# Square sums of the query heads on GpSimd instead of TensorE, in a two-layer decoder trunk on one Trainium2 core

## The chip, the core and the metric

The kernel runs on one core of a Trainium2 chip. A core has five engines that run side by side and meet only at semaphores: TensorE (PE; matrix products into PSUM banks; its weight loads are listed as PEld), VectorE (DVE), ScalarE (ACT), GpSimd (POOL) and SyncE (SP, which here only issues transfers). The metric is the device time of one launch in microseconds (us); lower is better.

## The reference, cut to what matters

Two layers work on x of 256 tokens by 2048 channels. Layer 0 holds a pooling mixer and block attention (MoBA) side by side, layer 1 holds sparse attention with an indexer (DSA) and a convolution module. Each layer projects a normalised, modulated x by a wide weight matrix. The change touches one thing in it, the root mean square norm of each query head over its 128 channels:

```
def _rms(x, g):
    x32 = x.astype(jnp.float32)
    y = x32 * lax.rsqrt(jnp.mean(x32 * x32, axis=-1, keepdims=True) + EPS)
    return (y * g.astype(jnp.float32)).astype(x.dtype)

    q = _rms(q.reshape(B_, S, N_HEADS, HEAD_DIM), moba_qn[e])   # layer 0; 8 heads of 128
    q = _rms(q.reshape(B_, S, N_HEADS, HEAD_DIM), dsa_qn[o])    # layer 1; 8 heads of 128
```

So for each of 2 x 8 heads and each of 256 tokens the sum of 128 squares is needed. It scales a row of the attention scores, so it is not needed before the first scores.

## The kernel before, in words

**Slabs.** All projections are cut into 141 slabs of 128 output channels. SP loads a slab as two halves of 512 KB (`load_slab`, L297 and L301). ACT rounds each half to the upper part `whi` (`hi`, L496), DVE subtracts to get the lower part `wlo` (`lo`, L1204), and TensorE forms a slab from 16 x 3 = 48 products of 256 columns (`slab`, L835 to L837; `slab_v`, L980 to L983, for keys and values) into one of two PSUM banks `Z[0]`, `Z[1]`, in turn. ACT and DVE work `AHEAD` = 2 slabs in front of TensorE. Between its slab work DVE also adds the modulation units `acc` (L1214, L1231), which SP streams from HBM.

**Order.** Each engine has its own list, written out by hand, which it goes through strictly in order; a wait holds back everything behind it on that engine. The first 12 slabs of layer 0 are worked together into six banks (`unsplit_chunk`); four of them are query heads 0 to 3. Slabs 12 to 15 are query heads 4 to 7 of layer 0, slabs 16 to 23 its keys, 24 to 31 its values. In layer 1 slabs 85 to 92 are the query heads, 93 to 100 the keys, from 101 on the values.

**Query heads.** ACT copies a query head with its channels on the partitions (tokens in the free dimension) from PSUM to `X` (L534, L658), squares it into a tile of 128 x 256 (L536, L659), and so frees the bank (`z_free`, for heads 0 to 3 `q_read`). For slabs 12 to 15 and 85 to 92 the square goes to `T[w % 2]`; heads 0 to 3 of layer 0 take `T[0]`, `T[1]`, `SG[0]`, `SG[1]`. TensorE then sums over the 128 partitions: a product for each half of the tokens, with the squares as weights and a column of ones (`qk_stats`, L943, called behind the next slab; L1093 for heads 0 to 3, in front of slab 13). The result is a column of bank `M` with the tokens on the partitions, and `qk_stat` is raised.

**Who reads the sums.** At the first value slab (24, 101) DVE waits for all 8 heads and computes the reciprocal roots of queries and keys (`rsqrt`, L1261 to L1273). Attention follows.

**GpSimd** has little to do: it clears the accumulators (`clear`, L391), issues some transfers (L413, L425, L432, L460), scales the position bias (`slopes`, L399), and adds squares of the new x at the end of layer 0 (L420). Its helper `own` issues an instruction and then waits for its completion.

**The small records.** One fp32 product shows as two records in the trace, so a head's two sums show as four (x4). Slabs' products show as one record each.

Of the kernel before, what the change touches and what calls it, by code (L numbers as in the profile page):

```python
# [11 lines left out]
P = 128  # L12
# [3 lines left out]
KC = D_MODEL // P  # L16
HC = HALF // P
QT = SEQ // P
# [81 lines left out]
def build(nc, xT, params, pool_w, w_slabs, ada_units, x1_dram, outT):  # L100
    ctx = ExitStack()
    with ctx:
# [49 lines left out]
        rc = sb("rc", [P, 16])  # L152
        psum = [ctx.enter_context(nc.psum_tensor(f"bank{i}", [P, 512], F32)) for i in range(8)]
# [41 lines left out]
        qk_stat = sem("qk_stat")  # L195
# [169 lines left out]
        def _(pool):  # L365
# [26 lines left out]

            def slopes(layer, heads=range(HC)):
# [38 lines left out]
            pool.dma_start(PW, pool_w).then_inc(pw_in, 16)  # L432
            clear(6)
# [26 lines left out]
            pool.dma_start(KI[IDX_DIM:2 * IDX_DIM, :], KW[0:IDX_DIM, :]).then_inc(ki_in, 16)  # L460
            pool.wait_ge(mask_ready, 1)
# [14 lines left out]
        def _(act):  # L476
# [54 lines left out]
            def evict_qk(w, t, q0, kind, layer):  # L531
# [3 lines left out]
                               Z[w % 2][:, 0:SEQ], ACT.Copy, scale=gain)  # L535
                act.activation(T[:, w % 2, :], Z[w % 2][:, 0:SEQ], ACT.Square).then_inc(z_free[w % 2], 1)  # L536

            def evict_k(w, k0):
                pair = (w - k0) // 2
                if (w - k0) % 2:  # L540
# [3 lines left out]
                                   bank[:].rearrange("p (a b) -> p a b", a=QT), ACT.Copy)  # L544
                    if pair:
                        b = (k0 + pair - 1) % 2
                        act.wait_ge(z_free[b], (k0 + 1 - b) // 2 + 1 + 2 * ((pair - 1) // 2 + 1))
# [113 lines left out]
            act.wait_ge(qk_stat, 4)  # L661
# [152 lines left out]
        def _(pe):  # L814
# [124 lines left out]
            def qk_stats(w, t, q0):  # L939

                pe.wait_ge(z_free[w % 2], bank_uses(w, t) + 2)
                for q in range(QT):
                    ins = mm(M[:, bass.ds(q * KC + now(w, t) - q0, 1)], T[:, w % 2, q * P:(q + 1) * P],  # L943
                             ones[:, 0:1], start=True, stop=True)
                ins.then_inc(qk_stat, 1)

# [136 lines left out]
            def slab_stat(q0):  # L1083
                def step(w, t):
                    slab_h(w, t)
                    qk_stats(w - 1, t, q0)
                return step

            slab_h(12, None)
            for i in range(4):  # L1090
                pe.wait_ge(q_read, i + 1)
                for q in range(QT):
                    ins = mm(M[:, q * KC + i:q * KC + i + 1], (T, SG)[i // 2][:, i % 2, q * P:(q + 1) * P],  # L1093
                             ones[:, 0:1], start=True, stop=True)
                ins.then_inc(qk_stat, 1)
# [708 lines left out]
```

## Time and profile before

| | |
|---|---|
| median of 3 runs | 983.06 us (979.67 to 984.81) |
| span of the profiled execution (first to last instruction) | 977.3 us |
| TensorE busy | 942.7 us (96%) |
| VectorE busy | 822.4 us (84%) |
| ScalarE busy | 422.5 us (43%) |
| GpSimd busy | 63.5 us (6%), 76 instructions |
| mean granted TensorE clock | 0.991 of full speed |
| DMA | 261.26 MB, mean 267 GB/s |

The span runs from the first to the last instruction of one execution; that execution's own launch time is not given apart from it, and the three timed runs lie 2.4 to 7.5 us above the span. Products of TensorE overlap in the records: a slab product has a record of 0.28 us but a new one starts every 0.12 us. For TensorE the start times are therefore read, not the durations. The granted clock is 1.00 at 2.4 GHz and 0.50 at 1.2 GHz.

### The profile page before, as it was taken

What the parts mean: (1) busy time and instruction counts of PE and PEld (TensorE: products, weight loads), DVE (VectorE), ACT (ScalarE), POOL (GpSimd) and SP (SyncE); (2) the same over time, 40 slices, a digit from 0 to 9 for tenths busy, and PEclk for the clock granted to TensorE, in tenths of its full rate; (3) what the DMA queues carried; (4) which work ended last, traced back from release to release, by engine and by line L of the source; (5) the groups of instructions that cost most, each with busy time, mean ns of one, the idle gap of its engine ahead of it and who ended that gap; (6) DMA issues with size and microseconds to landing.
All of it is one profiled execution on the core that took longest, in us unless ns stands there. A gap on an engine that the chain in (4) does not pass through costs nothing.

```text
span 977.3 us, 18750 instructions
## 1 busy us (share of the span) xinstructions
PE 942.7 (96%) x7042; PEld 908.3 (93%) x7042; DVE 822.4 (84%) x1256; ACT 422.5 (43%) x726; POOL 63.5 (6%) x76
## 2 busy tenths in 40 slices
PE   2999999999999999999999999999999999999998
PEld 2887889999998999999999999999999989998887
DVE  5887968887999778999887999888999986879964
ACT  2220125444655444444444444444556655743331
POOL 1000000010110000132100000000011100000000
PEclk9999998999999999999999999999999999999999
DMA  9999988888876878899959555544455445587962
GB/s 366 409 399 399 379 298 319 293 329 330 325 286 233 294 260 312 322 370 377 339 176 321 193 176 189 175 151 140 164 175 193 172 163 203 199 315 288 360 227 75
DMA packets 77666, 261.26 MB, mean 267 GB/s; under 512 B 7952, under 2 KB 8592, under 8 KB 77344
## 3 DMA queue, kind: packets, MB, share of 16 engines
q1 hardware_dynamic: 72384, 240.90, 67.5%
q10 hardware_dynamic: 2880, 10.49, 2.7%
q0 software_dynamic: 2336, 8.98, 2.6%
q8 instruction: 43, 0.70, 0.3%
q14 instruction: 23, 0.19, 0.1%
HBM read 256.07 MB, written 4.19 MB: 266 GB/s over the span
## 4 chain that ended last, share of the span: by engine, by line
PE 72%; DVE 19%; DMA 4%; issue 2%; ACT 2%; SPq 1%; DVEq 0%; ACTq 0%
PE bank L835 13%; PE bank L836 13%; PE bank L837 13%; PE bank L856 6%; DVE wlo L1204 5%; PE bank L893 4%; PE bank L980 4%; DVE acc L1214 4%; PE bank L983 4%; PE bank L982 4%; PE bank L854 3%; DMA Y<-ada_units 3%; DVE Y L1431 2%; PE bank L927 2%; DVE acc L1234 1%
## 5 line engine op out<-in xcount | busy, mean ns | idle before, releaser
L496 ACT ACTIVATE whi<-raw 128x1024 fp32r<-128x1024 f32 x256 | 270.1, 1060 | 382.3 <-PE bank L837 217.0
L1204 DVE TENSOR_TENSOR wlo<-raw,whi 128x1024 fp32r<-128x1024 f32 x256 | 312.0, 1234 | 74.9 <-ACT whi L496 73.6
L835 PE MATMUL bank<-hhi,whi 128*128 128x256 f32 x912 | 263.8, 289 | 2.5 <-ACT T L741 0.9
L836 PE MATMUL bank<-hlo,whi 128*128 128x256 f32 x912 | 259.3, 284 | 0.0
L837 PE MATMUL bank<-hhi,wlo 128*128 128x256 f32 x912 | 259.1, 284 | 0.0
L1214 DVE SCALAR_TENSOR_TENSOR acc<-ada,cact,acc 128x1024 f32<-128x1024 f32 x144 | 187.4, 1302 | 23.9 <-DMA ada<-ada_units 12.6
L835 PEld LDWEIGHTS bank<-hhi,whi 128*128 128x128 f32 x912 | 176.2, 193 | 5.3 <-issue 3.1
L836 PEld LDWEIGHTS bank<-hlo,whi 128*128 128x128 f32 x912 | 176.2, 193 | 0.1
L837 PEld LDWEIGHTS bank<-hhi,wlo 128*128 128x128 f32 x912 | 176.1, 193 | 0.0
L980 PE MATMUL bank<-whi,hhi 128*128 128x256 f32 x512 | 146.7, 287 | 0.0
L982 PE MATMUL bank<-whi,hlo 128*128 128x256 f32 x512 | 144.9, 283 | 0.0
L983 PE MATMUL bank<-wlo,hhi 128*128 128x256 f32 x512 | 144.9, 283 | 0.0
L980 PEld LDWEIGHTS bank<-whi,hhi 128*128 128x128 f32 x512 | 98.2, 192 | 0.8 <-issue 0.7
L1431 DVE SCALAR_TENSOR_TENSOR Y<-U,par,Y 128x256 f32<-128x256 f32 x240 | 98.6, 481 | 0.0
L982 PEld LDWEIGHTS bank<-whi,hlo 128*128 128x128 f32 x512 | 98.3, 192 | 0.1
L983 PEld LDWEIGHTS bank<-wlo,hhi 128*128 128x128 f32 x512 | 98.2, 192 | 0.0
L856 PE MATMUL bank<-both_g,whi 128*128 128x512 f32 x256 | 89.9, 399 | 0.0
L893 PE MATMUL bank<-X,raw 128*128 128x256 f32 x384 | 86.5, 387 | 1.6 <-DMA raw<-w_slabs 1.5
L893 PEld LDWEIGHTS bank<-X,raw 128*128 128x128 f32 x384 | 74.2, 195 | 12.2 <-issue 1.8
L835 PE MATMUL bank<-both_g,whi 128*128 128x256 f32 x256 | 73.1, 286 | 0.0
L836 PE MATMUL bank<-both_g,whi 128*128 128x256 f32 x256 | 72.5, 283 | 0.0
L837 PE MATMUL bank<-both_g,wlo 128*128 128x256 f32 x256 | 72.4, 283 | 0.0
(195 smaller groups left out, 1220.2 us busy)
## 6 DMA issues: line engine op xcount, KB each, us to landing
raw<-w_slabs SPq DMA_DIRECT2D x260, 512.0 KB, 4.5
ada<-ada_units SPq DMA_DIRECT2D x160, 512.0 KB, 6.6
raw<-w_slabs ACTq DMA_DIRECT2D x20, 512.0 KB, 7.0
V<-ada_units SPq DMA_DIRECT2D x16, 512.0 KB, 9.7
Y<-ada_units SPq DMA_DIRECT2D x16, 512.0 KB, 11.3
X<-xT SPq DMA_DIRECT2D x1, 2048.0 KB, 12.6
x_dram<-X POOLq DMA_DIRECT2D x4, 512.0 KB, 8.5
outT<-X POOLq DMA_DIRECT2D x3, 512.0 KB, 4.9
```

What stands on the lines that cost most here:

```text
L496: act.activation(whi[:, slot], raw[:, slot], ACT.Copy).then_inc(hi_done, 1)
L835: mm(out, whi[:, s, k, :], ahi[:, c, :], start=(c == 0), stop=False)
L836: mm(out, whi[:, s, k, :], alo[:, c, :], start=False, stop=False)
L837: last = mm(out, wlo[:, s, k, :], ahi[:, c, :], start=False, stop=(c == KC - 1))
L856: last = mm(out[:], whi[:, s, k, :], flat(both_g[:, c]), start=(c == 0), stop=(c == KC - 1), skip_group_check=True)
L893: last = mm(wide(s), raw[:, slot, k, :], X[:, c, :], start=(c == 0 and s % 2 == 0), stop=(c == KC - 1), skip_group_check=True)
L980: mm(out, hhi[:, c, tokens], upper, start=(c == 0 and q == 0), stop=False, skip_group_check=True)
L982: mm(out, hlo[:, c, tokens], upper, start=False, stop=False, skip_group_check=True)
L983: last = mm(out, hhi[:, c, tokens], lower, start=False, stop=(c == KC - 1), skip_group_check=True)
L1204: dve.tensor_tensor(wlo[:, s], source, whi[:, s].bitcast(F32), ALU.subtract)\
L1214: dve.scalar_tensor_tensor(acc[:, p % 2, :], unit_at(first + u), cact[:, bass.ds(k, 1)], acc[:, p % 2, :], ALU.mult, ALU.add).then_inc(ada ...
L1431: ins = dve.scalar_tensor_tensor(Y[:, j, :], U[:, j, k:k + SEQ], par[:, wcol:wcol + 1], Y[:, j, :], ALU.mult, ALU.add)
```

## The change

The sums over the partitions leave TensorE. For each query head GpSimd runs one `partition_all_reduce` (add) in place on the 128 x 256 tile of squares, waits for it, and issues two transfers, one for each half of the tokens, that move 128 numbers of partition 0 (512 bytes) into one column of a new SBUF tile `qsum`, 4 bytes into each of 128 partitions. Their landing raises one of four semaphores `q_sum`, one for each tile of squares (`T[0]`, `T[1]`, `SG[0]`, `SG[1]`). ACT waits for that semaphore before it overwrites a tile of squares, where it waited before only for the bank or (once, L661) for `qk_stat`. DVE waits for all `q_sum` at slabs 24 and 101 and reads `qsum` where it read bank `M`. In GpSimd's list the eight heads of layer 0 stand between the load of `PW` and `clear(6)`, those of layer 1 between the transfer to `KI` and `slopes(1)`.

```diff
+        qsum = sb("qsum", [P, 2, QT, HC])
...
-        qk_stat = sem("qk_stat")
+        q_sum = [sem(f"q_sum{i}") for i in range(4)]
...
+            def q_stats(layer, h, squared, home):
+                own(pool.partition_all_reduce(squared, squared, P, bass.bass_isa.ReduceOp.add))
+                for q in range(QT):
+                    pool.dma_start(qsum[:, layer, q, h:h + 1], squared[0:1, q * P:(q + 1) * P]).then_inc(q_sum[home], 16)
...
             pool.dma_start(PW, pool_w).then_inc(pw_in, 16)
+            for h in range(4):
+                pool.wait_ge(q_read, h + 1)
+                q_stats(0, h, (T, SG)[h // 2][:, h % 2, :], h)
+            for w in range(WIDE[0], K0):
+                pool.wait_ge(z_free[w % 2], w // 2 + 2)
+                q_stats(0, w - Q0, T[:, w % 2, :], w % 2)
             clear(6)
...
+            for w in range(Q1, K1):
+                pool.wait_ge(z_free[w % 2], w // 2 + 2)
+                q_stats(1, w - Q1, T[:, w % 2, :], w % 2)
             pool.wait_ge(mask_ready, 1)
             slopes(1)
...
@@ evict_qk (ACT)
+                h = w - q0
+                if layer == 0 or h >= 2:
+                    uses = (h - 2) // 2 if layer == 0 else 3 + h // 2
+                    act.wait_ge(q_sum[w % 2], 16 * QT * uses)
                 act.activation(T[:, w % 2, :], Z[w % 2][:, 0:SEQ], ACT.Square).then_inc(z_free[w % 2], 1)
@@ evict_k (ACT)
+                    if k0 == K0 and not pair:
+                        act.wait_ge(q_sum[2], 16 * QT)
+                        act.wait_ge(q_sum[3], 16 * QT)
@@ heads 0 to 3 (ACT)
-            act.wait_ge(qk_stat, 4)
             evict_qk(12, None, Q0, "q", 0)
@@ TensorE
-            def qk_stats(w, t, q0):
-                pe.wait_ge(z_free[w % 2], bank_uses(w, t) + 2)
-                for q in range(QT):
-                    ins = mm(M[:, bass.ds(q * KC + now(w, t) - q0, 1)], T[:, w % 2, q * P:(q + 1) * P],
-                             ones[:, 0:1], start=True, stop=True)
-                ins.then_inc(qk_stat, 1)
...
             slab_h(12, None)
-            for i in range(4):
-                pe.wait_ge(q_read, i + 1)
-                for q in range(QT):
-                    ins = mm(M[:, q * KC + i:q * KC + i + 1], (T, SG)[i // 2][:, i % 2, q * P:(q + 1) * P],
-                             ones[:, 0:1], start=True, stop=True)
-                ins.then_inc(qk_stat, 1)
             slab_h(13, None)
-            qk_stats(12, None, Q0)
-            slab_stat(Q0)(14, None)
+            slab_h(14, None)
             pool_product(0)
-            slab_stat(Q0)(15, None)
+            slab_h(15, None)
...
             for w in range(86, K1):
-                slab_stat(Q1)(w, None)
+                slab_h(w, None)
                 logits(w - 86)
@@ attention_step (DVE)
-                    dve.wait_ge(qk_stat, HC * (layer + 1))
+                    for home, uses in enumerate((3 + 4 * layer, 3 + 4 * layer, 1, 1)):
+                        dve.wait_ge(q_sum[home], 16 * QT * uses)
-                    rsqrt(2 * layer + 1, 2 * KC, M[:, 0:2 * KC], P, ksum[:])
+                    rsqrt(2 * layer + 1, 2 * KC, qsum[:, layer, :, :], P, ksum[:])
```

## Rows read from the trace of the kernel before

**Rows 1.** Page, part 4: the chain that ended last, share by engine

```profile
PE 72%; DVE 19%; DMA 4%; issue 2%; ACT 2%; SPq 1%; DVEq 0%; ACTq 0%
```

**Rows 2.** Waits of PE, 140 to 240 us: who for whom, us, times, longest

```profile
PE bank L1093 <- ACT T L659: 1.0, 1, 1.0
```

**Rows 3.** Windows: stretch, length, busy us of PE, PEld, DVE, ACT, POOL, clock, DMA share

```profile
146.90:150.90 4.00, 2.98 (x20) 2.53 (x18) 2.79 (x3) 4.00 (x12) 0.00 (x0) 0.86 0.86 342
150.90:156.70 5.80, 5.80 (x28) 5.80 (x29) 5.63 (x6) 1.84 (x5) 0.00 (x0) 0.51 0.94 335
...
206.70:208.30 1.60, 1.60 (x16) 1.60 (x16) 1.50 (x2) 1.06 (x1) 0.00 (x0) 1.00 0.97 366
...
480.00:485.00 5.00, 4.78 (x41) 4.59 (x40) 2.19 (x10) 1.92 (x5) 1.43 (x2) 0.93 1.02 413
...
618.00:681.00 63.00, 63.00 (x501) 60.23 (x500) 54.99 (x108) 27.32 (x42) 0.00 (x0) 1.00 0.44 153
```

**Rows 4.** Timeline of PE: start us, us, instruction, [idle before <-releaser]

```profile
146.74 0.28 PE L836 MATMUL bank<-hlo,whi 128*128 128x256 f32 x1
146.86 0.28 PE L837 MATMUL bank<-hhi,wlo 128*128 128x256 f32 x1
...
150.88 0.56 PE L835 MATMUL bank<-hhi,whi 128*128 128x256 f32 x1
...
156.58 0.31 PE L837 MATMUL bank<-hhi,wlo 128*128 128x256 f32 x1
...
165.45 0.50 PE L943 MATMUL bank<-ones,T 128*128 128x1 f32 x4
165.81 1.97 PE L955 MATMUL bank<-Y,V 128*128 128x256 f32 x8
167.43 0.47 PE L835 MATMUL bank<-hhi,whi 128*128 128x256 f32 x1
...
206.50 1.84 PE L927 MATMUL bank<-ones,acc 128*128 128x1 f32 x16
...
624.57 0.50 PE L943 MATMUL bank<-ones,T 128*128 128x1 f32 x4
624.99 0.49 PE L1041 MATMUL bank<-KW,QI 64*128 64x128 f32 x2
```

**Rows 5.** Timeline of ACT: the square of head 0

```profile
147.61 0.44 ACT L659 ACTIVATE T<-bank 128x256 f32<-128x256 f32 x1
```

**Rows 6.** Timeline of DVE, 145 to 202 us

```profile
145.99 2.67 DVE L1214 SCALAR_TENSOR_TENSOR acc<-ada,cact,acc 128x1024 f32<-128x1024 f32 x2 [2.04 <-DMA ada<-ada_units]
...
154.66 1.22 DVE L1204 TENSOR_TENSOR wlo<-raw,whi 128x1024 fp32r<-128x1024 f32 x1
...
171.84 1.23 DVE L1204 TENSOR_TENSOR wlo<-raw,whi 128x1024 fp32r<-128x1024 f32 x1 [1.70 <-ACT whi L496]
...
178.04 1.23 DVE L1204 TENSOR_TENSOR wlo<-raw,whi 128x1024 fp32r<-128x1024 f32 x1 [1.25 <-ACT whi L496]
...
199.08 2.35 DVE L1204 TENSOR_TENSOR wlo<-raw,whi 128x1024 fp32r<-128x1024 f32 x2
```

**Rows 7.** POOL: two groups by line (busy us, mean ns), one line's durations (ns min/median/max)

```profile
L420 POOL TENSOR_TENSOR SP<-SP,T 128x256 f32<-128x256 f32 x13 | 17.8, 1369 | 56.5 <-ACT T L691 56.5
L413 POOL DMA_DIRECT2D V<-xT x2 | 1.1, 575 | 29.3 <-PE bank L1028 29.3
L399 POOL TENSOR_SCALAR DS<-MK x8: 1169/1172/2082, 713.6 to 779.3; 128x384 f32<-128x384 f32 x8
```

**Rows 8.** Timeline of DVE at two instructions that run beside one of POOL

```profile
404.56 3.15 DVE L1214 SCALAR_TENSOR_TENSOR acc<-ada,cact,acc 128x1024 f32<-128x1024 f32 x2
...
713.44 2.66 DVE L1204 TENSOR_TENSOR wlo<-raw,whi 128x1024 fp32r<-128x1024 f32 x2
```

**Rows 9.** DMA issues of POOL: count, KB each, median us from issue to landing

```profile
U<-xT POOLq DMA_DIRECT2D x2, 512.0 KB, 8.8
...
KI<-KW POOLq DMA_DIRECT2D x1, 64.0 KB, 2.6
```

More of the change, by code:

```diff
@@ L1081, in _ @@
             unsplit_chunk(15)
[L1083 to L1087, printed above, removed]
-            slab_h(12, None)
-            for i in range(4):
-                pe.wait_ge(q_read, i + 1)
-                for q in range(QT):
-                    ins = mm(M[:, q * KC + i:q * KC + i + 1], (T, SG)[i // 2][:, i % 2, q * P:(q + 1) * P],
-                             ones[:, 0:1], start=True, stop=True)
-                ins.then_inc(qk_stat, 1)
+            slab_h(12, None)
             slab_h(13, None)
-            qk_stats(12, None, Q0)
-            slab_stat(Q0)(14, None)
+            slab_h(14, None)
             pool_product(0)
-            slab_stat(Q0)(15, None)
+            slab_h(15, None)
             for w in range(K0, V0):
                 slab_v(w, K0, keys=True)
-                if w == K0:
-                    qk_stats(w - 1, None, Q0)
                 if w < K0 + 2:
@@ L1158, in _ @@
                 if w == K1:
-                    qk_stats(w - 1, None, Q1)
                     logits(w - 86)
@@ L1261, in rsqrt @@
                     seq(dve.tensor_scalar(parts[:, :, HC:KC], keys, 1.0 / count, EPS, ALU.mult, ALU.add))
-                    a, src = parts[:, :, 0:HC], src.rearrange("p (q n) -> p q n", q=QT)[:, :, 0:HC]
+                    a = parts[:, :, 0:HC]
                     settle()
```

## The prediction

> **What bounds the kernel now.** I read the chain of waits first: TensorE holds 72% of it, DVE 19% [rows 1]. Then TensorE's waits in the stretch where the change begins: one only, 1.0 us, on ACT's squares of head 0 [rows 2]. So from 140 to 240 us TensorE is the bound, with a product started every 0.12 us (146.74 to 146.86) [rows 4]; a slab of 48 takes 5.8 us. The windows then show what the eye misses in the busy shares: while the sums of heads 0 to 3 run, the granted clock is 0.86, and in the 5.8 us behind them 0.51, which is the 1.2 GHz level [rows 3]. In layer 1 (618 to 681 us) TensorE is busy all the time and DVE for 54.99 of 63.00 us [rows 3]. What TensorE no longer issues is thus saved as long as DVE and the new waits keep up; those two are the question.
>
> **What goes, layer 0.** The last product of slab 12 starts at 146.86, so slab 13 could start at 146.98; it starts at 150.88 [rows 4]. That is 3.9 us, one wait and 16 one-column products with their doubled records. Then come 26 steps of slab 13 up to 156.58, 5.70 us where 26 x 0.12 = 3.1 would do: 2.6 us for the low clock. Four more heads are summed behind slabs 13 to 16, each from 165.45 to 165.81 or alike, 0.36 us: 1.4 us. Together 7.9 us.
>
> **What goes, layer 1.** Eight times from 624.57 to 624.99, 0.42 us [rows 4]: 3.4 us.
>
> **What comes: the custom instruction.** No row shows a reduction over partitions. From below it cannot beat a pass over 256 numbers per partition; the nearest row is GpSimd's own addition of two 128x256 tiles, 1.37 us [rows 7], and I take 1.4 us. From above: if the sum passes through the engine like eight such additions in a row, 8 x 1.37 = 11 us. For each transfer GpSimd's issue costs 0.58 us [rows 7], and I add 0.1 us for the completion wait: 1.4 + 0.1 + 1.15 = 2.65 us a head. A landing takes 2.6 us for 64 KB in a calm stretch (DMA share 0.44), 8.8 us for 512 KB in a full one [rows 3, 9]; here the share is 0.85 to 0.94 and the piece tiny, but 128 pieces of 4 bytes. I take 3.5 us, with 2.6 and 8.8 as ends.
>
> **The new wait that counts.** Head 0's squares are ready at 147.61 + 0.44 = 148.05 [rows 5]. Reduced 149.5, second transfer issued at 150.2, landed 153.7; with the ACT square of slab 12 (0.4) and two hand-overs bank Z[0] is free at about 154.6. Without the sums TensorE has finished slab 13 at 146.98 + 5.8 = 152.8, so it waits 1.9 us for slab 14. Behind ACT's waiting square stand its copies of slab 15's weights, which DVE does not reach before the pooling work behind 154.66 [rows 6]: no cost. The clock: 1.6 us of 16 one-column products at 206.7 left it at 1.00, the 4 us from 146.9 brought it down, the 5 us from 480 to 0.93 already inside [rows 3]. A gap of 1.9 us is like the first, so I charge nothing; if it falls all the same, 2.6 us. The later ones: head h of layer 0 is issued by 148.1 + 2.65 (h + 1), head 4 lands at about 164.3 and head 5 at 167. Their tiles are wanted by slab 14's and 15's squares, whose banks TensorE needs back only at slabs 16 (about 167.9) and 18. No wait. Slab 14 then ends at 154.6 + 5.8 = 160.4, not 165.45. With the other three sums that makes 7.9 - 1.9 = 6.0 us by slab 17.
>
> **What DVE lets through.** Slab 20's second half starts at 206.50 - 24 x 0.12 = 203.6 on TensorE; its lower part is written at 199.08 + 1.2 = 200.3 [rows 4, 6]: 3.3 us in hand. From 151 us to there DVE has only 1.70 + 1.25 us idle, both waiting for ACT [rows 6], which TensorE's earlier pace moves up. So TensorE can gain at most 3.3 + 2.95 = 6.3 us here, less what GpSimd takes from DVE. That price stands in two rows: beside the longest `slopes` (2.08 us, median 1.17; 384 numbers read) DVE's pair of subtractions took 2.66 us and not 2.35, 0.31 us [rows 6 to 8]; beside a two-input addition (512 read) a pair of units took 3.15 and not 2.67, 0.48 us. By numbers read, 256 cost about 0.2 us; eight heads 1.6 us (3.8 at 0.48). Layer 0 keeps 6.3 - 1.6 = 4.7 us. In layer 1 DVE's 8.0 us idle covers 3.4 + 1.6 us, ACT's wait for the tile of two heads ago has 7 us for each slab against 2.65, and DVE's wait at slab 101 comes long after. GpSimd's own list suffers nothing: it is idle in both places, and what stands behind is `clear(6)` and the bias, not due until about 208 us and 713 us.
>
> **Two rules of the Trainium skill that speak against the change.** The trace has GpSimd and DVE losing parts of a microsecond beside each other, 0.31 and 0.48 us [rows 8]. The skill's page SBUF — State Buffer, section "Who interferes with whom", says more: the pair of ports they share is an exclusive lock, held for the whole instruction; the other engine stands still. The trace does not agree: an addition of 1.37 us cost DVE 0.48. It is rival three.
> No row here prices a sum over partitions. The GPSIMD Engine Reference, section "Cross-partition — where GPSIMD wins", gives 247,699 ns for a partition-axis reduction of [128, 2048]; an estimate by it for 256 columns is 31 us a head, and by it the sum would be rival four's, about 1320 us. The same page, section "Instruction dispatch", has a first call of loaded code pay about 6 us; the sum stays the same if that falls into GpSimd's idle time before the first head.
>
> **Sum.** 4.7 + 3.4 = 8.1 us less. Both reckonings are differences inside the profiled execution (span 977.3 us); put on the median of 983.06, which is 5.8 us above that span, they give 975.0 us. The forecast's own range is 968 to 980.
>
> **Rivals.**
> 1. *The landing eats layer 0's gain.* With 8.8 us from issue to landing Z[0] is free at 159.5, about the 159.6 of before; TensorE has stood 6.7 us, the clock falls and 2.6 us are lost again; 1.4 us of sums remain, so layer 0 loses about 1 us, layer 1 gains 3.4: 980.6 us. For it: the full DMA engines, 4-byte pieces. Against: 2.6 us at KI. A reduction of 3 us does nearly the same.
> 2. *The custom instruction is slow (slower than before).* Place: squares of slab 14, which wait for head 4, fifth in GpSimd's line; TensorE needs that bank at 173.7 as of before. It decides from 148.1 + 5 (t + 1.25) - 0.6 + 3.5 + 0.4 = 173.7, t = 3.2 us, on. At t = 11: head 4 lands at 212.3, slab 16 is 39 us late. In layer 1 the first square is ready at about 626.5 (624.6 and 2 us for ACT) and one more follows every 7.1 us, the eighth at 676; at 12.25 us a head it has to wait for head 5, 626.5 + 6 x 12.25 + 2.9 = 703: 26 us. 983 + 65 = 1048 us. For it: nothing bounds it in the trace. Against: nothing in one pass over 256 columns resembles eight.
> 3. *DVE stands still for the whole reduction.* Eight times 1.4 = 11.2 us against 6.3 in hand makes layer 0 4.9 us longer; in layer 1 11.2 against 8.0 idle is 3.2 more: 991 us.
> 4. *A reduction that goes through the numbers one by one, 31 us a head* (the page's rule above). Eight heads with their issues take 261 us. DVE's wait at the first value slab comes some 80 us behind head 0 in layer 0 (12 slabs of 5.8 us and the small products between them) and some 100 us in layer 1 (16 slabs): 180 + 160 us longer, about 1320 us. For it: only that the sum over partitions has no row. Against: each of GpSimd's rows of this size is under 2.1 us [rows 7].
>
> **How the numbers follow.** Forecast 55%, rival one 25%, two 10%, three 8%, four 2%. A measurement of this kernel tells 0.5%, 4.9 us, from no change. Of the forecast's case a tenth (its upper end, 978 to 980) falls within that; faster 0.50, within 0.30, slower 0.20. The range for 8 in 10 takes the forecast's and rival one's: 968 to 988.
>
> **What would show it.** No L943 or L1093; slab 13 starts at 147.0 and the clock stays at 1.00 up to 160; TensorE's longest new wait is 1 to 3 us before slab 14, on ACT's square, and that on a transfer. GpSimd shows 16 custom instructions whose spacing to the first transfer is 1.4 us; DVE's L1204 mean stays below 1.27 us. If slab 16 starts later than 173.7, rival two or one holds; if L1204 stretches by more than 1 us beside GpSimd, rival three. An unchanged start of slab 16 and a gain in layer 1 alone would make the forecast wrong by its larger term.

## The result, and the profile after

| | before | after |
|---|---|---|
| median of 20 runs | 981.02 us (976.79 to 984.81) | 984.30 us (981.22 to 991.29) |
| ratio, 95% interval | | 1.0036 [1.0021, 1.0052] |
| span of the profiled execution | 977.3 us | 982.7 us |
| mean granted TensorE clock | 0.991 | 0.991 |

The kernel became 3.5 us slower, where 8 us less were forecast. The predicted range held the time; the sign was wrong. TensorE issues less, and the kernel is no faster for it.

The page of the kernel after: part 1, engine busy, and part 4, the chain that ended last.

```profile
span 982.7 us, 18682 instructions
PE 937.6 (95%) x6978; PEld 901.3 (92%) x6978; DVE 835.7 (85%) x1256; ACT 422.5 (43%) x726; POOL 118.2 (12%) x124
...
PE 56%; DVE 30%; DMA 7%; issue 4%; ACT 2%; SPq 1%; DVEq 0%; ACTq 0%
```

DVE is busy 835.7 us where it was 822.4, though the change gives it no work; its share of the chain rises from 19% to 30% [rows 1]. The waits of TensorE from 140 to 240 us (who for whom: us, times, longest) say the same. [rows 2] shows one before, 1.0 us, on ACT; a second, 0.8 us for ACT's `U` at 140 us, is in both kernels:

```profile
PE bank L968 <- DVE Y L1362: 3.1, 2, 2.5
PE bank L993 <- DVE wlo L1201: 2.9, 2, 1.5
PE bank L856 <- DVE wlo L1201: 2.6, 2, 2.0
PE bank L856 <- ACT U L672: 1.0, 2, 0.8
```

The first three, 8.6 us, are for DVE: for the pooled operand `Y` and for lower parts of weights. The windows of the kernel after, with the columns of [rows 3]:

```profile
146.90:150.90 4.00, 2.85 (x24) 2.64 (x23) 3.25 (x3) 4.00 (x12) 2.16 (x2) 1.00 0.68 274
150.90:156.70 5.80, 4.91 (x28) 4.91 (x29) 5.70 (x4) 3.07 (x6) 5.43 (x6) 0.71 0.63 200
156.70:178.00 21.30, 17.25 (x132) 16.29 (x130) 20.85 (x24) 8.66 (x14) 16.54 (x18) 1.00 0.71 243
178.00:212.00 34.00, 31.46 (x251) 30.84 (x250) 32.89 (x40) 14.42 (x32) 0.78 (x2) 1.00 0.86 310
618.00:681.00 63.00, 63.00 (x491) 59.28 (x490) 61.65 (x109) 29.01 (x44) 30.17 (x25) 1.00 0.50 164
```

TensorE's first new wait is not the one forecast, before slab 14 on ACT's square. It stands in the middle of slab 13, for DVE's lower part of the second half, and the clock is 0.71 right behind it (150.90 to 156.70), where 1.00 was forecast:

```profile
151.79 0.52 PE L856 MATMUL bank<-hhi,whi 128*128 128x256 f32 x1 [2.05 <-DVE wlo L1201]
```

From 156.70 to 178.00 DVE is busy 20.85 of 21.30 us with 24 instructions; before, 17.86 us for the same number:

```profile
156.70:178.00 21.30, 21.30 (x174) 21.09 (x173) 17.86 (x24) 9.89 (x15) 0.00 (x0) 1.00 0.85 303
```

So the instructions of DVE grew longer. Which ones, the timelines show. GpSimd first, after:

```profile
148.43 1.81 POOL L395 PARTITION_ALL_REDUCE T<-T  x1 [19.32 <-ACT T L681]
...
151.87 1.74 POOL L395 PARTITION_ALL_REDUCE T<-T  x1
...
155.03 1.82 POOL L395 PARTITION_ALL_REDUCE SG<-SG  x1
...
158.26 1.76 POOL L395 PARTITION_ALL_REDUCE SG<-SG  x1
...
161.43 1.74 POOL L395 PARTITION_ALL_REDUCE T<-T  x1
...
164.59 1.96 POOL L395 PARTITION_ALL_REDUCE T<-T  x1
...
168.84 2.27 POOL L395 PARTITION_ALL_REDUCE T<-T  x1 [0.91 <-ACT T L555]
...
174.47 2.39 POOL L395 PARTITION_ALL_REDUCE T<-T  x1 [1.99 <-ACT T L555]
```

And DVE, after, in the same stretch:

```profile
146.35 1.28 DVE L1211 SCALAR_TENSOR_TENSOR acc<-ada,cact,acc 128x1024 f32<-128x1024 f32 x1 [3.06 <-DMA ada<-ada_units]
148.38 2.22 DVE L1211 SCALAR_TENSOR_TENSOR acc<-ada,cact,acc 128x1024 f32<-128x1024 f32 x1 [0.74 <-DMA ada<-ada_units]
150.53 3.47 DVE L1201 TENSOR_TENSOR wlo<-raw,whi 128x1024 fp32r<-128x1024 f32 x2
153.92 3.31 DVE L1211 SCALAR_TENSOR_TENSOR acc<-ada,cact,acc 128x1024 f32<-128x1024 f32 x2
...
158.29 1.61 DVE L1349 TENSOR_TENSOR SP<-U 128x542 f32<-128x542 f32 x1
159.94 0.69 DVE L1356 SCALAR_TENSOR_TENSOR Y<-SP,U 128x512 f32<-128x512 f32 x1
...
160.93 1.63 DVE L1362 TENSOR_TENSOR Y<-SP,U 128x2 f32<-128x2 f32 x2
...
163.62 3.31 DVE L1211 SCALAR_TENSOR_TENSOR acc<-ada,cact,acc 128x1024 f32<-128x1024 f32 x2
...
167.99 0.71 DVE L1349 TENSOR_TENSOR SP<-U 128x542 f32<-128x542 f32 x1
...
169.49 1.47 DVE L1356 SCALAR_TENSOR_TENSOR Y<-PTs,U 128x512 f32<-128x512 f32 x1
...
171.25 0.24 DVE L1362 TENSOR_TENSOR Y<-PTs,U 128x4 f32<-128x4 f32 x2
...
175.13 3.25 DVE L1201 TENSOR_TENSOR wlo<-raw,whi 128x1024 fp32r<-128x1024 f32 x2
```

Eight reductions, and eight rows of DVE that are too long, each where a reduction runs. Against the same forms undisturbed (1.28, 0.71, 0.69 and 0.24 above; 2.35 and 2.67 in [rows 6]) the excess is 0.94, 1.12, 0.64, 0.90, 1.39, 0.64, 0.78 and 0.90 us: 7.3 us, 0.91 for each reduction. The reductions grow as well: the first six take 1.74 to 1.96 us, the last two 2.27 and 2.39.

In layer 1 the same is seen in one group, the taps of the convolution, after. Columns: busy us, mean ns, idle before.

```profile
L1428 DVE SCALAR_TENSOR_TENSOR Y<-U,par,Y 128x256 f32<-128x256 f32 x240 | 105.3, 506 | 0.0
```

The same group before:

```profile
L1431 DVE SCALAR_TENSOR_TENSOR Y<-U,par,Y 128x256 f32<-128x256 f32 x240 | 98.6, 481 | 0.0
```

105.3 less 98.6 is 6.7 us for eight reductions, 0.84 each. It lies in DVE's idle time: 61.65 of 63.00 us are busy there, 54.99 before [rows 3].

**Where the time went.** A shift table says at which slab the kernel after falls behind. I read it from the start of DVE's subtraction for the first half of each slab: start in the kernel, less its start at slab 12, less the same difference in the kernel before. It rests on one profile of each kernel. Negative is earlier.

| kernel | slab 16 | 20 | 28 | 52 | 84 | 124 | ratio of the timed runs |
|---|---|---|---|---|---|---|---|
| after | +6.95 | +4.73 | +3.80 | +3.79 | +8.56 | +6.22 | 1.0036 [1.0021, 1.0052] |
| e1_no_sums | -0.07 | -2.27 | -0.54 | -0.54 | -0.94 | -3.60 | 0.9973 [0.9956, 0.9990] |
| e3_no_reduce | +0.06 | -3.09 | -4.01 | -4.03 | -3.55 | -6.23 | 0.9969 [0.9953, 0.9986] |
| e4_write_only | -0.13 | -2.72 | -3.16 | -3.16 | -1.52 | -4.17 | 0.9951 [0.9935, 0.9966] |
| e12_read_copy | +3.29 | +1.41 | +2.15 | +2.15 | +3.02 | +0.35 | 0.9994 [0.9972, 1.0017] |
| e2_own_tiles | +7.59 | +5.36 | +6.09 | +6.09 | +6.26 | +4.14 | 1.0067 [1.0042, 1.0092] |
| e5_twice | +8.18 | +9.80 | +11.18 | +11.18 | +12.63 | +17.94 | 1.0189 [1.0166, 1.0213] |
| e6_layer0 | +5.51 | +3.36 | +2.42 | +2.42 | +2.86 | +3.18 | 1.0055 [1.0033, 1.0077] |
| e7_layer1 | +0.64 | -0.80 | -0.80 | -0.80 | +1.51 | -0.69 | 0.9989 [0.9974, 1.0004] |
| e8_late_sums | -0.08 | -3.17 | -4.11 | -4.12 | -3.24 | -3.25 | 0.9988 [0.9972, 1.0003] |
| e11_both | -0.03 | -3.02 | -3.95 | -3.96 | -3.25 | -5.44 | 0.9959 [0.9941, 0.9977] |
| e13_side_eight | +5.04 | +2.80 | +3.47 | +3.47 | +4.10 | +4.12 | 1.0045 [1.0019, 1.0072] |
| e14_side_four | +2.59 | -0.55 | -0.93 | -0.93 | +0.60 | +0.61 | 1.0000 [0.9978, 1.0021] |
| e15_late_side | +5.15 | +2.91 | +1.98 | +1.98 | +4.72 | +4.74 | 1.0025 [1.0000, 1.0050] |

In the kernel after 3.80 us are lost by slab 28 (layer 0) and 2.3 won in layer 1 (slab 84 to 124). Some 4.8 more are lost between slabs 52 and 84, where nothing of the change runs; `e6_layer0` loses 0.4 there. The trace shows on what: the clock of 460 to 480, 480 to 500 and 500 to 530 us is 0.91, 0.91 and 0.94 in the kernel after, 1.00, 0.91 and 1.00 before. By length times what is missing that is 3.6 us more lost, and TensorE has a new wait of 2.0 us for DVE's `X` there. Why the clock fell twice more is not shown; `e4`, with 0.91 and 0.94 in the last two of these stretches, has one such fall more than before and runs well below it.

The table is coarse to a microsecond or two in another way: it rests on one execution each, and for `e3`, `e6`, `e8` and `e11` that was the fastest one timed. The ratios decide.

A second table shows DVE alone, from the start of its first subtraction for slab 12 to the end of the third pooled operand (before: the rows at 186.16). How much later that operand and TensorE's product on it come than before is again counted from slab 12.

| kernel | GpSimd in it | DVE busy | DVE idle | operand | product |
|---|---|---|---|---|---|
| before | nothing | 41.35 | 12.28 | 0 | 0 |
| e3_no_reduce | transfers only | 41.24 | 9.31 | -3.07 | -4.11 |
| e4_write_only | 8 `memset` | 41.24 | 9.68 | -2.71 | -3.16 |
| e8_late_sums | nothing | 41.20 | 9.26 | -3.17 | -4.21 |
| e12_read_copy | 8 pairs of copies | 45.25 | 9.80 | +1.42 | +0.38 |
| e14_side_four | 4 reductions | 44.20 | 8.89 | -0.54 | -0.93 |
| e13_side_eight | 8 reductions | 47.79 | 8.65 | +2.81 | +1.77 |
| e15_late_side | 8 reductions | 47.84 | 8.71 | +2.91 | +1.87 |
| e6_layer0 | 8 reductions | 48.59 | 8.41 | +3.37 | +2.33 |
| after | 8 reductions | 48.43 | 9.94 | +4.73 | +3.69 |
| e2_own_tiles | 8 reductions | 48.96 | 10.03 | +5.36 | +4.32 |
| e5_twice | 16 reductions | 54.94 | 8.49 | +9.80 | +8.76 |

DVE does the same work in all of them. Without an instruction of GpSimd that reads SBUF it takes 41.2 to 41.4 us, with four reductions 2.9 us more, with eight 6.4 to 7.6 more, with sixteen 13.6 more: 0.7 to 0.95 us each. In the kernel after 1.8 us of the lateness are DVE's longer waits for modulation units before 148.4 us (3.06 + 0.74, before 2.04); `e6` does not have them, so they are not laid to the change.

### The profile page after: what moved, and what is told of

Same layout as the page of the kernel before. It is cut to its first block, busy times and chain, and to the rows that moved or that the text cites. A ratio compares the mean times of both kernels' runs of the same rounds, so it can differ in the third digit from the quotient of the medians.

```text
span 982.7 us, 18682 instructions
## 1 busy us (share of the span) xinstructions
PE 937.6 (95%) x6978; PEld 901.3 (92%) x6978; DVE 835.7 (85%) x1256; ACT 422.5 (43%) x726; POOL 118.2 (12%) x124
## 4 chain that ended last, share of the span: by engine, by line
PE 56%; DVE 30%; DMA 7%; issue 4%; ACT 2%; SPq 1%; DVEq 0%; ACTq 0%
PE bank L856 9%; PE bank L857 9%; PE bank L858 9%; DVE wlo L1201 9%; DVE acc L1211 7%; PE bank L877 6%; DVE Y L1428 6%; DMA ada<-ada_units 6%; PE bank L914 4%; PE bank L993 3%; PE bank L995 3%; PE bank L996 3%; PE bank L875 3%; PE bank L948 2%; DMA Y<-ada_units 1%
## 5 line engine op out<-in xcount | busy, mean ns | idle before, releaser
L1211 DVE SCALAR_TENSOR_TENSOR acc<-ada,cact,acc 128x1024 f32<-128x1024 f32 x144 | 189.8, 1318 | 30.4 <-DMA ada<-ada_units 19.4
L1428 DVE SCALAR_TENSOR_TENSOR Y<-U,par,Y 128x256 f32<-128x256 f32 x240 | 105.3, 506 | 0.0
```

What stands on the lines that cost most here:

```text
L1211: dve.scalar_tensor_tensor(acc[:, p % 2, :], unit_at(first + u), cact[:, bass.ds(k, 1)], acc[:, p % 2, :], ALU.mult, ALU.add).then_inc(ada ...
L1428: ins = dve.scalar_tensor_tensor(Y[:, j, :], U[:, j, k:k + SEQ], par[:, wcol:wcol + 1], Y[:, j, :], ALU.mult, ALU.add)
```

## The experiments

Each was timed in 5 rounds beside the kernel before. `e1`, `e3`, `e4` and `e12` leave the sum over the partitions out and `e5` makes it 128 times too large, so their query norms are not the reference's. Differences in microseconds are taken from the ratios, since the kernel before ran beside each group anew. The diffs are cut to their core.

**Is it the reduction, the transfers, or the saving itself?** `e1_no_sums` has neither reductions nor transfers; `e3_no_reduce` keeps the transfers and the waits for them.

```diff
 # e3_no_reduce (e1_no_sums also replaces the two transfers by a semaphore increment)
-                own(pool.partition_all_reduce(squared, squared, P, bass.bass_isa.ReduceOp.add))
```

> The changed kernel without any sums: no reduction, no transfer, no products of TensorE; qsum holds a constant (the norms of the query heads are left out). It prices what TensorE stood to gain. Theory P (GpSimd's reductions take the port from DVE and make DVE late) and theory W (ACT waits for the transfers to land) both expect 7 to 11 us below the kernel before, a ratio of 0.989 to 0.993, slab 13 starting right behind slab 12 and no drop of the clock. Rival H (the time of the one-column products was hidden anyway, DVE or the loads being the next bound): under 3 us below.

> The changed kernel without the 16 reductions, with its 32 transfers and all waits (the sums are left out; partition 0's squares are moved). Theory P: DVE's two-input instructions keep their 1.21 and 1.28 us and nearly all of e1's gain comes, 6 to 10 us below before. Theory W: the reductions were 1.8 of 4 to 6 us from square to landing, so most of the wait stays, 0 to 3 us below before.

Measured: 979.38 and 977.10 us against 980.84. With no sums at all the kernel is only 2.6 us faster, so 8 us were not there to be won: both theories had expected 7 to 11, and rival H holds. And without the reductions alone the loss becomes a gain: 0.9969 against 1.0036, 6.6 us. `e3` itself is 3.0 us below the kernel before, less than theory P expected and at the edge of theory W's range; so its time alone does not tell the two apart. DVE's busy time does (41.24 us, as without sums), and `e2` below. The transfers and their waits are not what costs. How the gain is capped shows at the third pooling product. Before, its operand from DVE, and the product:

```profile
186.16 0.24 DVE L1365 TENSOR_TENSOR Y<-SP,U 128x8 f32<-128x8 f32 x2
```

```profile
187.50 1.89 PE L955 MATMUL bank<-Y,V 128*128 128x256 f32 x8
```

DVE has it ready at 186.40, TensorE comes at 187.50: 1.1 us in hand, and 2.95 us of DVE's idle time before it [rows 6]. More than 1.1 + 2.95 = 4.05 us can't be won there. `e3`, DVE and then TensorE:

```profile
182.60 0.24 DVE L1361 TENSOR_TENSOR Y<-SP,U 128x8 f32<-128x8 f32 x2
```

```profile
182.90 1.99 PE L967 MATMUL bank<-Y,V 128*128 128x256 f32 x8 [2.52 <-DVE Y L1361]
```

TensorE waits 2.52 us for DVE there, and at slab 28 the kernel is 4.01 us ahead. The same row after, where TensorE's list is the same and DVE is late:

```profile
190.45 1.99 PE L968 MATMUL bank<-Y,V 128*128 128x256 f32 x8 [2.54 <-DVE Y L1362]
```

In `e1` the wait was longer, and the clock of 178 to 212 us fell to 0.90 (it is 1.00 in the kernel before); of 2.27 us won by slab 20, 0.54 are left at slab 28:

```profile
187.75 3.78 PE L967 MATMUL bank<-Y,V 128*128 128x256 f32 x8 [3.47 <-DVE Y L1361]
```

```profile
178.00:212.00 34.00, 30.53 (x225) 29.56 (x224) 30.78 (x38) 14.15 (x31) 0.58 (x1) 0.90 0.85 308
```

**Is it that GpSimd is busy, or that it reads?** `e4_write_only` puts a `memset` of 1920 columns, about as long as a reduction, in its place; `e12_read_copy` two copies of 384 columns from `D`.

```diff
 # e4_write_only
-                own(pool.partition_all_reduce(squared, squared, P, bass.bass_isa.ReduceOp.add))
+                own(pool.memset(both_g[:].rearrange("p a b t -> p (a b t)").bitcast(F32)[:, 0:1920], 1.0))
 # e12_read_copy: in its place, twice
+                own(pool.tensor_copy(scr[:], D[:]))
```

> As the changed kernel, but each reduction is replaced by a memset of 1920 columns of an idle tile, which keeps GpSimd busy for about as long (951 ns for 1024 columns, so 1.8 us) and reads nothing; transfers and waits stay (the sums are left out). Theory P in its form 'the reduction's reads collide with DVE's second SBUF input': DVE keeps its durations, and the time is e3's within 2 us (head 0 lands 1.8 us later). If the mere time from square to landing, or GpSimd's work of any kind, were the cost: the changed kernel's time within 1.5 us.

> The changed kernel with each reduction replaced by two copies of the 384 columns of D into a scratch tile, which keep GpSimd busy for about as long as a reduction (0.5 us for 256 columns, so 0.75 each) and read SBUF, unlike e4's memset (the sums are left out). Theory P (any GpSimd instruction that reads SBUF takes time from DVE's two-input instructions): 2 to 6 us above e4 and its DVE durations stretched. If only the custom instruction does it: e4's time within 1.5 us, DVE's durations as in before.

Measured: `e4` 976.48 us, 4.8 below the kernel before; `e12` 980.45 us, 4.2 above `e4`. The taps in `e4`, then the copies and the taps in `e12` (busy us, mean ns):

```profile
L1428 DVE SCALAR_TENSOR_TENSOR Y<-U,par,Y 128x256 f32<-128x256 f32 x240 | 98.6, 479 | 0.0
```

```profile
L396 POOL COPY scr<-D 128x384 f32<-128x384 f32 x16 | 16.6, 1036 | 52.6 <-ACT T L557 34.2 <-ACT T L683 18.2
```

```profile
L1430 DVE SCALAR_TENSOR_TENSOR Y<-U,par,Y 128x256 f32<-128x256 f32 x240 | 102.5, 495 | 0.0
```

In `e4` GpSimd is busy for as long as in the kernel after (1.72 us each), and DVE keeps pace with `e3` (slab 20 -2.72 and -3.09); its taps take what they took before; in `e12` they are longer again, 495 ns, and DVE is busy 3.9 us more up to the third pooled operand. So of the kinds tried the two that read SBUF (reduction and copy) slow DVE, and the one that only writes does not. `e12` also has a longer wait: TensorE stood 4.2 us once for a square of ACT whose transfer was late, so the 4.2 us between the two times are not DVE's alone. In `e4` such a wait was 3.1 us, and the kernel is still 4.8 us faster than before. On the reading side the Trainium skill, page SBUF — State Buffer, section "Who interferes with whom", agrees: a DVE instruction with two SBUF inputs contends with a GpSimd instruction that reads SBUF, not with one that only writes it.

**How much for each reduction?** `e2_own_tiles` gives the squares of layer 0 tiles of their own, so that ACT waits for no landing; `e5_twice` is `e2` with each reduction issued twice.

```diff
 # e2_own_tiles: q_stats and ACT's squares, layer 0
-                q_stats(0, h, (T, SG)[h // 2][:, h % 2, :], h)
+                q_stats(0, h, QI[:, h, :], 2)
-                q_stats(0, w - Q0, T[:, w % 2, :], w % 2)
+                q_stats(0, w - Q0, (T[:, 0, :], T[:, 1, :], KW[:], KI[:])[w - 12], 2)
 # e5_twice: as e2, and
                 own(pool.partition_all_reduce(squared, squared, P, bass.bass_isa.ReduceOp.add))
+                own(pool.partition_all_reduce(squared, squared, P, bass.bass_isa.ReduceOp.add))
```

> The changed kernel with a tile of its own for each of layer 0's eight squares (QI, T, KW, KI, all idle there), so that ACT waits for no landing in layer 0; reductions and transfers as they are. Theory W: the 6.3 us that ACT waited go and TensorE's waits in slabs 14 to 18 with them, 4 to 6 us below the changed kernel (ratio to before 0.994 to 0.998). Theory P: DVE loses about 0.9 us a reduction as before and the pooling work is as late; within 1.5 us of the changed kernel (ratio to before 1.002 to 1.005).

> The kernel with own tiles (e2) in which every reduction is issued twice in a row on its tile (the sums come out 128 times too large). It doubles the suspected cost alone, since ACT waits for no landing in layer 0. Theory P (each reduction takes about 0.5 to 0.9 us from DVE where DVE has none to give): 6 to 14 us above e2. Theory L (a fixed cost of the new path, such as loading the instruction's code or the transfers): under 2 us above e2.

Measured: `e2` 987.10 us (+6.6), `e5` 998.91 us. The landing wait, rival one, is refuted as the cause: without it nothing is won. That `e2` is worse than after is not shown; their intervals overlap from 1.0042 to 1.0052. Sixteen more reductions cost 12 us by the ratios (8.6 to 15.3 by their intervals), 0.75 each. DVE is busy 850.0 us in `e5` and 836.7 in `e2`: 13.3 us, 0.83 each.

**Which layer?** `e6_layer0` has the change in layer 0 only, `e7_layer1` in layer 1 only; the other layer keeps `qk_stats` on TensorE.

```diff
 # e7_layer1, from the kernel before; e6_layer0 is its mirror
             pool.dma_start(KI[IDX_DIM:2 * IDX_DIM, :], KW[0:IDX_DIM, :]).then_inc(ki_in, 16)
+            for w in range(Q1, K1):
+                pool.wait_ge(z_free[w % 2], w // 2 + 2)
+                q_stats(1, w - Q1, T[:, w % 2, :], w % 2)
...
-                slab_stat(Q1)(w, None)
+                slab_h(w, None)
```

> The change in layer 0 alone, layer 1 summed by TensorE as before. After e1 (all sums away: 2.7 us less) and e3/e4 against the changed kernel (reductions: 7 to 8 us more) theory P expects layer 0 to carry the larger part of the loss, since there DVE is the last to be ready for the pooling products: 2 to 5 us above before. If layer 1 carried it: within 1 us of before.

> The change in layer 1 alone. TensorE gives up 8 x 0.42 us; DVE has 8.0 us idle there of which eight reductions take about 6.7 (a run of 7 or 8 convolution taps grew by 0.8 us beside each). Theory P: the gain is just eaten or nearly, from 2 us below to 1 us above before. If the loss sat here: 3 us or more above before.

Measured: `e6` 986.02 us (+0.55%, interval 0.33 to 0.77), `e7` 979.33 us (-0.11%, -0.26 to +0.04). The loss sits in layer 0. It is larger in the timed runs of `e6`, 5.4 us, than in its profile, 2.4 at slab 28 and 3.2 at slab 124; the profiled execution was the fastest of them. Layer 1 gives about 1 us, which its interval can't tell from none; between slabs 84 and 124 its profile wins 2.2 us. The two add up to +0.44%, near the whole change's 0.36%.

**Is TensorE's saving in layer 0 worth anything while DVE is late?** `e13_side_eight` is the kernel before, with its sums left on TensorE, and eight reductions on the side in layer 0 whose result nobody reads or waits for; `e14_side_four` has the first four of them.

```diff
 # e13_side_eight, from the kernel before (the run calls own(...) through a helper, side_reduce)
             pool.dma_start(PW, pool_w).then_inc(pw_in, 16)
+            for h in range(4):
+                pool.wait_ge(q_read, h + 1)
+                own(pool.partition_all_reduce(QI[:, 0, :], D[:, 0:SEQ], P, bass.bass_isa.ReduceOp.add))
+            for w in range(WIDE[0], K0):          # not in e14_side_four
+                pool.wait_ge(z_free[w % 2], w // 2 + 2)
+                own(pool.partition_all_reduce(QI[:, 0, :], D[:, 0:SEQ], P, bass.bass_isa.ReduceOp.add))
```

> The kernel before, all its sums by TensorE, plus eight reductions by GpSimd in layer 0 at the places of the change, which read D and write the idle tile QI; no transfer, nobody waits for them. Theory Max (at the third pooling product TensorE waits for DVE; DVE has 1.1 us in hand there and 2.95 us idle before, 4.05 in all, and eight reductions take 7.8 us from it): TensorE is 3.8 us late from slab 28 on, as in the changed kernel, 3 to 5 us above before, though TensorE saved nothing. Theory Add (losses and savings simply add up): the changed kernel's loss plus the 4 us that it saved in layer 0, 7 to 9 us above before.

> As e13 with the first four reductions only (heads 0 to 3). Theory Max: 3.9 us taken from DVE's 4.05, so within 1 us of before. Theory Add: half of e13's loss, 3.5 to 4.5 us above before.

Measured: 985.34 us (1.0045) and 981.64 us (1.0000), against 982.31. Eight reductions beside a TensorE that keeps its sums cost 4.4 us by the ratios; the change in layer 0 (`e6`) costs 5.4, the whole change 3.5. If DVE's loss came on top of TensorE's time, `e13` would be 7 to 8 us late. It isn't: DVE is busy 6.4 us longer up to the third pooled operand but idle 3.6 us less, so the operand comes 2.8 us late; 1.1 us were in hand, and the product comes 1.8 us late. The 3.47 us at slab 28 have another 1.6 us in them, since the clock was low during that product:

```profile
190.34 3.59 PE L963 MATMUL bank<-Y,V 128*128 128x256 f32 x8 [2.74 <-DVE Y L1373]
```

The same product took 3.47 us in `e2` and 3.50 in `e12`, so their slab 28 has it too; in `e3` and after, behind waits of 2.52 and 2.54 us, it ran at full clock. TensorE's longest wait in `e13`, 140 to 240 us, is for the third pooled operand; the next, for head 0's square, is the one that was there before, now 1.8 us:

```profile
PE bank L963 <- DVE Y L1373: 2.7, 1, 2.7
PE bank L1101 <- ACT T L667: 1.8, 1, 1.8
```

`e14` closes it from the other side: its four reductions take 2.9 us of DVE, less than the slack, and nothing is lost.

**Can the saving be had without GpSimd?** `e8_late_sums` is the kernel before with heads 0 to 3 squared into `QI`, a tile that is free there, and their 16 products put in front of the third pooling product, where TensorE has DVE's slack to wait for anyway. `e15_late_side` adds the eight side reductions to it.

```diff
 # e8_late_sums, from the kernel before: the loop over i in range(4) moves from behind slab_h(12) to here
+                if w == K0 + 1:
+                    for i in range(4):
+                        pe.wait_ge(q_read, i + 1)
+                        for q in range(QT):
+                            ins = mm(M[:, q * KC + i:q * KC + i + 1], QI[:, i, q * P:(q + 1) * P],
+                                     ones[:, 0:1], start=True, stop=True)
+                        ins.then_inc(qk_stat, 1)
                 if w < K0 + 2:
                     pool_product(w - K0 + 1)
 # ACT: heads 0 to 3
-                act.activation((T, SG)[i // 2][:, i % 2, :], wide(8 + i), ACT.Square).then_inc(q_read, 1)
+                act.activation(QI[:, i, :], wide(8 + i), ACT.Square).then_inc(q_read, 1)
-            act.wait_ge(qk_stat, 4)
```

> The kernel before with one change of its own: heads 0 to 3 of layer 0 are squared into the idle tile QI and TensorE sums them not ahead of slab 13 but ahead of the third pooling product, where it would otherwise wait for DVE; GpSimd does nothing new. If the gain of e1 in layer 0 is the gap and the low clock at slab 13: 1 to 4 us below before, as far as DVE's pooling work lets it. If DVE holds TensorE back there whatever TensorE does: within 1 us of before.

> e8 (TensorE sums heads 0 to 3 late, 4.1 us ahead of before at slab 28 in its profile) plus the eight side reductions of e13. Theory Max: DVE sets the time, so the same as e13, 3 to 5 us above before, TensorE's saving being worth nothing. Theory Add: e13 less e8's gain, 3 to 4 us below e13.

(`e15` writes its reductions to `KI`, since `QI` is taken.) Measured: `e8` 979.21 us (0.9988), `e15` 983.99 us (1.0025). In the profile `e8` does what it should: the wait and the low clock at slab 13 are gone (clock 1.00 in both first windows), the 16 products take 1.84 us and TensorE then waits 0.15 us; 4.11 us are won by slab 28, the whole cap.

```profile
181.62 1.84 PE L1102 MATMUL bank<-ones,QI 128*128 128x1 f32 x16
183.62 1.99 PE L954 MATMUL bank<-Y,V 128*128 128x256 f32 x8 [0.15 <-DVE Y L1365]
```

The timed runs give less, 1.2 us with an interval that reaches zero. `e15` against `e8` is 3.6 us for eight reductions; at slab 28 it is 6.1. If DVE alone sets when TensorE can go on, `e15` and `e13` must be equally late at the third pooling product, though TensorE has 16 products less in front of slab 13 in `e15`. They are: +1.87 and +1.77 us. The 1.5 us between them at slab 28 are the clock: in `e15` the same product ran at full clock.

```profile
189.34 1.99 PE L962 MATMUL bank<-Y,V 128*128 128x256 f32 x8 [1.29 <-DVE Y L1373]
```

By the ratios `e15` is 2.0 us below `e13`, which their intervals (1.0000 to 1.0050, 1.0019 to 1.0072) can't tell from none.

**Is the gain given back to the load stream?** The loads of slabs 56 to 64 run with the DMA engines at 0.94 busy and more (440 to 480 us), and a gain there might end in a wait for data. `e9_light` is the kernel before with every modulation unit from slab 34 on loaded by half (the output of those units is not the reference's), `e10_light_late` the same on `e8`.

```diff
+                    if n >= FIRST + 48:
+                        sp.dma_start(unit_at(n + u)[:, 0:PIECE // 2], ada_units[bass.ds(unit, 1), :, 0:PIECE // 2]
+                                     .rearrange("a p n -> p (a n)")).then_inc(ada_in[unit_slot(n + u)], 16)
+                        continue
```

> The kernel before with a lighter stream: from slab 34 on each modulation unit is loaded with half of its 512 KB (the rest of the tile keeps old numbers, so the modulation of layer 1 is wrong in part). It is the partner of e10. TensorE is bound by its own work in that stretch, so 0 to 4 us below before under either theory.

> e8 (sums of heads 0 to 3 moved) with the same lighter stream as e9. In e8's profile TensorE was 3.8 us ahead of before at slab 20 and lost it again up to slab 63, where the loads run at 0.94 to 0.97 of the DMA engines and ACT waits 26 us for slabs instead of 12.5. Theory M (what TensorE gains before is given back waiting for HBM): with the lighter stream the gain stays, 3 to 5 us below e9. Theory N (the gain is lost elsewhere, in attention or by chance): 0 to 2 us below e9, as e8 was to before.

Measured: `e9` 977.38 us (0.9961 [0.9939, 0.9983]), `e10` 975.70 us (0.9954 [0.9935, 0.9972]). The lighter stream is worth 3.8 us by itself, so data are waited for somewhere; on top of it the late sums give 0.7 us by the ratios, no more than on the full stream. That the loads eat the gain is not supported; the intervals are too wide to exclude it.

**The version that the runs point to.** `e11_both` has `e8`'s late sums in layer 0 and the change itself in layer 1, where DVE has 8 us of idle time for it.

> e8's moved sums in layer 0 and the change (GpSimd) in layer 1 alone. If the two small gains add up: 2 to 3 us below before (ratio 0.997 to 0.998), better than both kernels. If the layer 1 part is nothing: as e8, about 1 us below.

Measured: 976.60 us against 981.24, 0.9959 [0.9941, 0.9977]: 4 us faster than the kernel before and 7.6 faster than the kernel after by the ratios. TensorE's waits from 140 to 240 us are down to 0.3 us for the third pooled operand, beside the 0.8 for ACT's `U` that was there.

## Why the prediction was wrong

**The step that failed** is "What DVE lets through", in both of its terms.

The limit was read at the wrong place. 3.3 us in hand at slab 20 plus 2.95 idle made 6.3; but DVE hands TensorE something earlier and tighter, the third pooled operand, with 1.1 us in hand. The limit was 4.05 us, and `e3` (4.01) and `e8` (4.11) reach just that at slab 28. Slabs' lower parts were looked at, the one operand between them was not.

The contention was sized at a quarter. 0.2 us for a reduction came from the longest `slopes` (0.31 us) scaled by numbers read. Measured: 0.91 in the rows of layer 0, 0.84 in layer 1, 0.75 by doubling. Eight of them are 7.3 us, not 1.6. So in the forecast's own form layer 0 is -4.05 + 7.3 = +3.3 us, where 6.3 - 1.6 = 4.7 us less was forecast; that one number turns the sign. The form is rough. Traced through, a late DVE also fills 1.14 us that it stood idle at 150 us before the change, ahead of the stretch that the prediction looked at, and what it is busy longer is 6.4 to 7.6 us; the product comes 1.8 us late in `e13` and 1.9 in `e15`, 2.3 in `e6`, and 3.7 in the kernel after, of which 1.8 are the longer waits for modulation units. That the form comes close to the +3.80 at slab 28 is in part luck. The idle time at 150 us, before:

```profile
150.93 1.22 DVE L1204 TENSOR_TENSOR wlo<-raw,whi 128x1024 fp32r<-128x1024 f32 x1 [1.14 <-ACT whi L496]
```

The upper bound that stood beside it, 0.48 a head, was too low as well: both bounds came from GpSimd's ordinary instructions, and the reduction does not behave like them. For those the price by numbers read was fair: the two copies of `e12` read 768 numbers and cost DVE 0.49 us a head (0.6 by that price), a reduction of 256 numbers costs 0.7 to 0.95.

The sign that was to show it was blunt: L1204's mean stayed below the 1.27 us named (1.241), though single pairs grew by 1.12 us. A mean of 256 hides eight.

**Layer 0's saving on TensorE (7.9 us)** was for the most part there where DVE kept pace. In `e3` and `e8` the clock of the two windows at slab 13 is 1.00 and the gap is gone; `e1` and `e3` come to the second pooling product, behind all eight sums of before, 6.8 and 6.7 us early. It could not be kept. In the kernel after that product comes 1.1 us late: TensorE had by then waited for DVE.

**Rows 2** were read as TensorE's only wait from 140 to 240 us. There was a second, 0.8 us for ACT's `U`; it is in the kernel after and in the others too and changes nothing.

**The landing wait** was sized fairly and did not matter. GpSimd's transfers of `T` land in 2.4 us at the median, those of `SG` in 4.0, where 3.5 were taken, and ACT waits three times, head 4's square first:

```profile
153.27 0.38 ACT L555 ACTIVATE T<-bank 128x256 f32<-128x256 f32 x1 [0.80 <-DMA qsum<-T]
159.54 0.38 ACT L555 ACTIVATE T<-bank 128x256 f32<-128x256 f32 x1 [1.59 <-DMA qsum<-T]
168.36 0.38 ACT L555 ACTIVATE T<-bank 128x256 f32<-128x256 f32 x1 [3.95 <-DMA qsum<-T]
```

The third was said not to come ("No wait"). `e2` removes all three and wins nothing.

**The custom instruction** takes 1.74 to 1.82 us for the first five heads of layer 0, where 1.4 were taken, and up to 3.06 at the end of layer 1. No run has it with DVE idle. Rivals two (from 3.2 us on) and four (31 us) fell.

**Layer 1** was forecast at -3.4 us. The profiles give -2.3 (after), -2.2 (`e7`) and -2.7 (`e1`, `e3`, `e4`) between slabs 84 and 124; the timed runs of `e7` -1.1 with an interval of 1.5 either way. The reason given for it, DVE's idle time as cover, held by a small margin: 6.7 of 8.0 us are used up.

**Rival three** (8% for 991 us) had the mechanism and the place, and the sign with them. It was oversized: DVE loses 0.91 us beside a reduction of 1.74 us and more, not all of it, and the reduction is stretched in its turn. The prediction read the rule of the SBUF page as an exclusive lock for the whole instruction. The Trainium skill's page says that of DVE's two-port mode; of a DVE instruction with two SBUF inputs it says that it contends, not for how long. Held for the whole instruction, eight reductions of 1.8 us would have cost DVE 14 us in layer 0; the trace has 7.3. What should have raised its chance stood in the prediction: an addition of 1.37 us cost DVE 0.48, a third of its length. By length and not by numbers read, eight reductions of 1.8 us would have been 5 us, above the slack of 4.05: from 0.5 us a head on layer 0 is a loss.

**What stays open.** Why the clock of the kernel after falls twice more between slabs 52 and 84 than before; the timed runs, at 3.5 us in all, do not need that loss, and it may be that execution's own. Why `e6` loses 5.4 us in the timed runs and 2 to 3 in its profile. And why a reduction takes 0.9 us of DVE's time and not its whole length.

## What to carry to other kernels

- Work moved from the bounding engine to an idle one is free only if that one does not slow a third. Before crediting the saving, find the slack of each engine that feeds the bound, at every operand it hands over, the small ones between the large too. Price the disturbance with an instruction of the kind that will run, or with a test run that only adds it, as `e13` does.
- GpSimd instructions that read SBUF beside DVE's two-input ones are paid for by DVE, 0.7 to 0.95 us for a reduction of 128x256 here; a `memset`, which only writes, was not. Put them where DVE is idle for that long.
- A gap of TensorE can often be closed by moving the work that makes it to where TensorE waits anyway: `e8` and `e11` took layer 0's saving that way, without the price: 1.2 us by the ratios (an interval from 2.7 us down to none) and, with layer 1's change, 4.0.

## What the runs showed of the hardware that was not expected

GpSimd has gaps where it goes over to the reduction and where it comes back from it. Its first reduction in layer 1 started at 630.46, 2.1 us after its square was ready at 628.36, and its first `slopes` of layer 0 came behind 11.25 us in which nothing that the profile shows was waited for. After, and the same `slopes` before, which follows its transfers (209.31 + 1.51) at once:

```profile
225.14 2.36 POOL L405 TENSOR_SCALAR DS<-D 128x384 f32<-128x384 f32 x2 [11.25 <-issue]
...
630.46 1.81 POOL L395 PARTITION_ALL_REDUCE T<-T  x1 [7.37 <-issue]
```

```profile
210.85 2.35 POOL L399 TENSOR_SCALAR DS<-D 128x384 f32<-128x384 f32 x2
```

The runs tie both gaps to the reductions. All seven kernels with reductions in layer 0 (after, `e2`, `e5`, `e6`, `e13`, `e14`, `e15`) have 9.6 to 11.9 us in front of that `slopes`; `e3`, `e4`, `e7`, `e11` and `e12`, which have none there, start it at once. In front of the first reduction of layer 1 the gap is 6.5 to 7.4 us in the five that have one, counted from the transfer to `KI`. Both were hidden here: DVE does not wait for GpSimd from 200 to 280 us, nor ACT for a landing in layer 1. The Trainium skill, GPSIMD Engine Reference, section "Instruction dispatch", has a first call of loaded code pay about 6 us. The second row fits that; of the way back, 11.25 us, the page says nothing. That either is code loading is inferred, no record names it. The first head of layer 0 showed no such wait, behind 19.32 us of idle time.
